# Decode attention over paged latents: pages turned by VectorE and scored in 32x32 tiles, with a fourth page buffer and loads shared by SyncE and GpSimd's gathers

## The reference, cut to what matters

```python
# cache_ckv (160, 128, 256), cache_kpe (160, 128, 32), page_table (8, 16)
c_past = cache_ckv[page_table].reshape(8, 2048, 256)
kpe_past = cache_kpe[page_table].reshape(8, 2048, 32)
s = einsum('bqhr,bkr->bhqk', q_lat, c_past) + einsum('bqhe,bke->bhqk', q_pe, kpe_past)
p = softmax(s * 96 ** -0.5)          # with the new token's own key beside the past ones
o_lat = einsum('bhqk,bkr->bqhr', p, c_past)
o = einsum('bhqr,rhv->bqhv', o_lat, w_uv);  x = x + o.reshape(b, n, 1024) @ w_o
```

## Time and profile before

| | |
|---|---|
| median of 3 executions | 2004.9 us (2004.75 to 2006.88) |
| the profiled execution | 2008.5 us, its span 2006.8 us |
| TensorE busy | 1965.1 us (98% of the span) |
| VectorE, ScalarE, GpSimd busy | 1280.1, 820.4, 132.3 us |
| mean granted TensorE clock | 0.988 of full |
| scores of request 0 done, scores of request 7 done | 1510.23 us, 1575.93 us of the span |

### The profile page before, as it was taken

How to read it: one execution, slowest core, us unless ns; L and a number is a source line. 1 busy time by engine, 2 the same in 40 slices (tenths; PEclk the granted TensorE clock), 3 DMA queues, 4 the chain that set the end, 5 groups by cost and what they waited for, 6 DMA issues and landing times.

```text
span 2006.8 us, 41571 instructions
## 1 busy us (share of the span) xinstructions
PE 1965.1 (98%) x17584; PEld 1878.2 (94%) x17584; DVE 1280.1 (64%) x1781; ACT 820.4 (41%) x1243; POOL 132.3 (7%) x231
## 2 busy tenths in 40 slices
PE   8999999998999999999999999999989999999998
PEld 7999999988999999999999999997656899999998
DVE  6445486697469577576875856655764349668474
ACT  5332233343245244355452534554654244345252
POOL 3002002010000000000000000000048000000000
PEclk9999999989999999999999999998999999999999
DMA  7233234864342322234322322231248422323222
GB/s 150 85 102 88 77 91 115 278 134 97 95 137 85 124 87 98 72 105 116 97 87 83 126 89 87 78 101 51 53 119 234 151 70 79 127 85 125 86 74 75
DMA packets 260625, 211.49 MB, mean 105 GB/s; under 512 B 42372, under 2 KB 235426, under 8 KB 260450
## 3 DMA queue, kind: packets, MB, share of 16 engines
q1 hardware_dynamic: 248528, 187.52, 31.6%
q0 software_dynamic: 6656, 13.69, 2.4%
q10 hardware_dynamic: 5266, 7.78, 1.2%
HBM read 195.22 MB, written 10.33 MB: 102 GB/s over the span
## 4 chain that ended last, share of the span: by engine, by line
PE 68%; DVE 3%; ACT 2%; issue 2%; SPq 1%; DMA 0%; DVEq 0%; ACTq 0%
PE ps L2459 25%; PE ps L2487 25%; PE ps L2388 6%; PE ps L2401 2%; PE ps L3034 1%; PE ps L2941 1%; PE ps L3190 1%; PE ps L3067 1%; SPq L637 1%; PE ps L3011 1%; PE ps L2835 1%; SPq L652 1%; DVE wl L1666 0%; DVE xl L1617 0%; DVE mx L2210 0%
## 5 line engine op out<-in xcount | busy, mean ns | idle before, releaser
L2388 PE MATMUL ps<-xh,wh 128*128 128x260 f32 x1088 | 286.9, 285 | 2.6 <-DVE xl L1617 1.4
L2388 PE MATMUL ps<-xl,wh 128*128 128x260 f32 x1088 | 283.7, 283 | 0.0
L2487 PE MATMUL ps<-xoh,wh 128*128 128x260 f32 x992 | 281.3, 284 | 1.3 <-DVE sq L1833 1.3
L2487 PE MATMUL ps<-xoh,wl 128*128 128x260 f32 x992 | 281.0, 283 | 0.0
L2487 PE MATMUL ps<-xol,wh 128*128 128x260 f32 x992 | 280.6, 283 | 0.0
L2459 PE MATMUL ps<-xh,wh 128*128 128x260 f32 x872 | 228.8, 284 | 0.6 <-DVE wl L1666 0.6
L1065 ACT ACTIVATE wh<-rw 128x1024 fp32r<-128x1024 f32 (+1 forms) x135 | 138.8, 1029 | 218.6 <-PE ps L2459 151.7
L2459 PE MATMUL ps<-xl,wh 128*128 128x260 f32 x872 | 227.0, 282 | 0.0
L2388 PE MATMUL ps<-xh,wl 128*128 128x260 f32 x1088 | 219.3, 283 | 0.0
L988 ACT ACTIVATE wh<-raw 128x1024 fp32r<-128x1024 f32 (+1 forms) x90 | 100.5, 1116 | 283.0 <-PE ps L2388 251.2
L2388 PEld LDWEIGHTS ps<-xh,wh 128*128 128x128 f32 x1088 | 205.6, 189 | 6.9 <-issue 3.9
(11 more groups left out here) (550 smaller groups left out, 4214.9 us busy)
## 6 DMA issues: line engine op xcount, KB each, us to landing
rw<-ffn_w_gate SPq DMA_DIRECT2D x33, 1024.0 KB, 5.3
rw<-ffn_w_up SPq DMA_DIRECT2D x33, 1024.0 KB, 7.9
rw<-ffn_w_down SPq DMA_DIRECT2D x12, 2048.0 KB, 7.7
raw<-ffn_w_gate SPq DMA_DIRECT2D x22, 512.0 KB, 3.8
raw<-ffn_w_up SPq DMA_DIRECT2D x22, 512.0 KB, 3.7
raw<-ffn_w_down SPq DMA_DIRECT2D x16, 704.0 KB, 4.8
rw<-ffn_w_down SPq DMA_DIRECT2D x6, 1536.0 KB, 6.6
cb<-cache_ckv SPq DMA_DIRECT2D x72, 128.0 KB, 3.9
```

The costliest lines, as they stand in the source:

```text
L2388: got = mm(ps[0:width, bank + half, 0:HALF], w[par_][:, k * width:k * width + width], src[:, k0 + k, half * HALF:half * HALF + HALF], star ...
L2487: got = mm(ps[:, bank + mat, T0], w[:, cols], src[:, j, k, :], start=first and k == 0 and m == 0 and s == 0, stop=k == 3 and m == 1, skip_ ...
```

## The change

* **Turning.** The 36 transposes of TensorE for each request and the nine copies out of PSUM go. VectorE turns the pages in SBUF with its own transpose, which works on 32x32 blocks: one instruction over 512 numbers a partition for the keys (into `kbT`) and four over 1024 numbers a partition for the latents (chunk c into `cbT[:, c-1]`, 64 of the 256 latent numbers each). The semaphore `d_t` now counts these.
* **Scoring.** A 32x32 block leaves 32 latent numbers on the partitions of each of four quarters, and each quarter holds other positions. So the scores are made of tiles with 32 rows and 32 columns, all 16 of the array: `past_scores(b, c)` issues 16 matmuls of 128 columns for the keys (c = 0) and 32 for each of the four latent chunks, 144 for a request. Each quarter of rows writes a PSUM bank of its own (banks 0 to 3, which request b+1 may write only when the exponential of request b has read them). The queries are needed on every quarter: GpSimd writes them to DRAM once and reads them back eight times (`dr_q`, `qrep`).
* **Order.** TensorE's order for a request is now: transposes of the probabilities, all scores of request b+1, weighted sum of request b. The copy of the turned probabilities moves from VectorE to ScalarE; ScalarE's copy of the weighted sum comes one request later.
* **Pages.** A page lies on 32 partitions with four positions on each, so that a partition receives 4 KB of latents or 512 bytes of keys. SyncE issues 8 latent pages and 4 key pages for a request; GpSimd gathers the others with indirect DMAs of four pages each (2 for latents, 3 for keys) whose row numbers it works out once from the page table.
* **Buffers.** A fourth latent buffer `cbw` lies over `wh[0]`, `wh[1]` and part of `wl[0]`. Therefore the splitting of the `w_o` blocks 0 and 1 leaves the prompt's steps 4 and 6 and comes with the blocks 2 and 3 at the end of the decode loop (`wide_hi`, `wide_lo`, into the first two page buffers). `uv` moves to `cbT` and is loaded when the last scores are done.

```diff
-            def turned(b, q):
-                dve.wait_ge(d_t, b * 9 + q + 1)
+            def turned(b, c):
+                if c == 0:
+                    dve.wait_ge(d_key[b % KB_BUFS], KEY_0[b % KB_BUFS] + (b // KB_BUFS + 1) * 16 * SP_KEYS)
+                    dve.wait_ge(d_gkey[b % KB_BUFS], (b // KB_BUFS + 1) * 16 * (NQ - SP_KEYS // NQ))
+                elif c == 1:
+                    dve.wait_ge(d_in[b % CB], IN_1 + (b // CB + 1) * 16 * SP_PG)
+                    dve.wait_ge(d_gin[b % CB], (b // CB + 1) * 16 * (NQ - SP_PG // NQ))
                 if b >= 1:
-                    dve.wait_ge(d_s, b)
-                copy(cbT[:, q // 4, (q % 4) * 512:(q % 4) * 512 + 512], ps[:, (0, 1, 7)[(b * 9 + q) % 3], :]).then_inc(d_td, 1)
+                    dve.wait_ge(d_s, (NCT + 1) * (b - 1) + c + 1)
+                if c == 0:
+                    V.transpose(kbT, kb[b % KB_BUFS].rearrange("p g e -> p (g e)")).then_inc(d_t, 1)
+                else:
+                    V.transpose(cbT[:, c - 1, :, :].rearrange("p q (g u) -> p g q u", u=HP),
+                                cb[b % CB][:, :, 2 * HP * (c - 1):2 * HP * c].rearrange("p g (q r) -> p g q r", q=2)).then_inc(d_t, 1)
...
             for b in range(NB):
-                dve.wait_ge(d_s, b + 1)
-                own(V.tensor_reduce(mb[:, b:b + 1], ps[:, 2 + b % 2, :], AX.X, ALU.max))
+                if b + 1 < NB:
+                    turned(b + 1, 0)
+                dve.wait_ge(d_s, (NCT + 1) * (b + 1))
+                own(V.tensor_reduce(mb[:, b:b + 1], ps[:, 0:NQ, 0:P], AX.XY, ALU.max))
                 ts(nmb[:, b:b + 1], mb[:, b:b + 1], -SCALE, None, ALU.mult).then_inc(d_m, 1)
                 if b + 1 < NB:
-                    turned(b + 1, 1)
-                    turned(b + 1, 3)
-                else:
-                    wide_lo(0)
-                dve.wait_ge(d_pt2, b + 1)
-                if b >= 1:
-                    dve.wait_ge(d_o, b)
-                copy(pbT[:, :, :], ps[:, 4, :].rearrange("p (m q) -> p m q", m=NQ)).then_inc(d_pe, 1)
+                    for c in range(1, NCT + 1):
+                        turned(b + 1, c)
+                if b >= NB - 2:
+                    wide_lo(b - NB + 2)
...
+            def past_scores(b, c):
+                if b == 0 and c == 0:
+                    pe.wait_ge(d_qr, 16 * (1 + 2 * NQ))
+                if b >= 1 and c == 0:
+                    pe.wait_ge(d_e, b)
+                pe.wait_ge(d_t, (NCT + 1) * b + c + 1)
+                for q in range(2 if c else 1):
+                    n = 2 * (c - 1) + q
+                    for a in range(NQ):
+                        rows = slice(HP * a, HP * a + HP)
+                        w, keys_ = (qrep[n // NQ][rows, n % NQ, b, :], cbT[rows, c - 1, q, :]) if c else (qpe[rows, b, :], kbT[rows, :])
+                        for j in range(NQ):
+                            got = mm(ps[HP * j:HP * j + HP, a, 0:P], w, keys_[:, P * j:P * j + P],
+                                     start=c == 0, stop=c == NCT and q == 1, skip_group_check=True)
+                got.then_inc(d_s, 1)
...
+            def gather(src, dst, b, g, arrived):
+                G.indirect_dma_start(dst[:, ROWS * g:ROWS * (g + 1), :].rearrange("p v r -> p (v r)"), None,
+                                     inp[src].rearrange("n (u v) r -> (n u) (v r)", v=ROWS),
+                                     bass.IndirectOffsetOnAxis(ap=rows_of[:, NQ * b + g:NQ * b + g + 1], axis=0)).then_inc(arrived, 16)
```

More of the change, by code:

```diff
@@ L922, in rope_rows, with number, keys, pages @@
                     sp.dma_start(qs[DN:DQ, 2 * (i % 2) + h, :], qq[r0:r0 + DR, NH // 2 + i // 2, 0:SEQ]).then_inc(a_qs[i % 2], 16)
[L924 removed]
+            numbers = {}
+            def number(b):
+                numbers[b] = [sp.value_load(pt[0:1, b * NPG + g:b * NPG + g + 1], min_val=0, max_val=NPOOL - 1) for g in range(SP_PG)]
+            def keys(b):
+                keys_free(sp, b)
+                for g in range(SP_KEYS):
+                    sp.dma_start(page(kb[b % KB_BUFS], g), inp["cache_kpe"][bass.ds(numbers[b][g], 1)].rearrange(
+                        "a (u v) r -> (a u) (v r)", v=ROWS)).then_inc(d_key[b % KB_BUFS], 16)
+            def pages(b):
+                latents_free(sp, b)
+                for g in range(SP_PG):
+                    sp.dma_start(page(cb[b % CB], g), inp["cache_ckv"][bass.ds(numbers[b][g], 1)].rearrange(
+                        "a (u v) r -> (a u) (v r)", v=ROWS)).then_inc(d_in[b % CB], 16)
+            sp.wait_ge(d_pt, 16)
             sp.wait_ge(q_ev, NQT)
@@ L943, in _ @@
             load(WO0 + 1, (WO0 + 1) % 2, wo[:, :, P:2 * P], KD)
-            caches()
-            sp.wait_ge(d_o, NB - 2)
+            for b in range(NB):
+                pages(b)
+                if b == 0:
+                    keys(0)
+                if b == 1:
+                    for m in range(AHEAD, NB):
+                        number(m)
+                if b + 1 < NB:
+                    keys(b + 1)
+            for d in range(2, 4):
+                load(WO0 + d, (WO0 + d) % 2, wo[:, :, d * P:d * P + P], KD)
+            sp.wait_ge(d_s, (NCT + 1) * NB)
             sp.dma_start(uv[:, :, :], uvd).then_inc(d_uv, 16)
-            for d in range(2, KD - 2):
+            for d in range(4, KD - 2):
                 load(WO0 + d, (WO0 + d) % 2, wo[:, :, d * P:d * P + P], KD)
@@ L3166, in _ @@
                 turned_probs(i, 3)
-                if not more:
-                    turned(0, 0)
                 turned_probs(i, 4)
-                if not more:
-                    turned(0, 1)
                 turned_probs(i, 5)
@@ L3218, in _ @@
+            for c in range(NCT + 1):
+                past_scores(0, c)
+            for b in range(NB):
                 pe.wait_ge(d_e, b + 1)
```

283 lines of the change are left out of this document (149 added, 134 removed).

## The result

The changed kernel takes 2032.8 us (median, 2030.2 to 2036.9) against 2005.9 for the kernel before on the same chip: ratio 1.0134, 95% interval 1.0111 to 1.0158. It is **1.3% slower**, where 17.4 us less were forecast. Its profiled execution took 2036.9 us, span 2035.0, against 2008.5 and 2006.8 before, so the traces differ by 28.2 us.

A forecast was written before the change was run, and what follows sets the result against it. TensorE was taken to bound the decode loop, VectorE after the change. Loop -20.5, start -0.5, tail +2.6, 1 given back: -17.4, so 1991.1 profiled and 1987.5 us as median; own range 1982 to 1994, over all 1981 to 2010.

The forecast's parts named there:

- the scores' price: Decode loop, TensorE: score records start 8 ns apart, so 0.5 us a chunk and 2.3 us for a request's scores.
- The packing: Score matmuls: 16 tiles of 32x32 work side by side, 8 ns a record, continued from one and four tiles.
- VectorE's chain: Decode round: maximum, four latent transposes, then TensorE's last chunk; sum 6.35 us, taken as 6.45, the new bound.
- the 20.5 us: Decode loop: gain forecast for the seven rounds between requests' last scores, 45.2 us instead of 65.7.
- TensorE before: Decode loop of the kernel before: TensorE sets the round, 9.37 us a request, 4.4 of it turning pages.
- close second bound: Decode loop of the kernel before: page loads bound next after TensorE, DMA share 0.83 at 234 GB/s.
- VectorE: Decode loop: VectorE's page transposes take 1.18 us a latent chunk, 4.7 for four, and 0.6 for the keys.
- Gathers: Page loads beside the loop: each GpSimd gather taken at 1.0 us, 0.54 the bound below.
- Start: Up to request 0's scores: done at 1509.7 against 1510.2, 0.5 us less, within 2 either way.
- Tail: Behind the last scores: uncovered wait, less filler before the `w_uv` product and four later steps, 2.6 us more.
- that the tiles do not pack: Rival, scores: records start 30 ns apart, round 11.3 us, 2026 us, slower; decides from 22 ns; chance 0.14.
- The falling clock: Rival, decode loop: TensorE idles and its clock falls to 1.2 GHz, round 8.6 us, 2005 us, same; chance 0.08.

The follow-up runs named there:

- few loads: Changed kernel without the latents' page loads of requests 4 to 7, their key pages loaded as before: 2020.3 us, ratio 1.0064.
- few scores: Changed kernel with 102 instead of 288 score records a request, three quarters of the latents' scores left out: 1993.8 us, ratio 0.9945.

## Why the prediction was wrong, step by step

* **The step that failed** is the scores' price: "records of 16 columns in four column tiles start eight in 0.06 us, 8 ns each, so they can be issued that fast", and from it 0.5 us a chunk and 2.3 us a request. It took a rate from a burst for a rate that lasts. The groups in the earlier trace rows are bursts of 8, 64 and 128 records, and 128 are exactly one packet; the loop has 324 records a round. One packet takes 3.47 us with the DMA engines idle and 7.04 to 9.4 in the changed kernel's stretches under loads, so 324 / 128 = 2.53 packets bound the round at 8.8 us with the first figure and 17.8 with 7.04. The first figure alone leaves 0.6 us a round of the 2.9 that were forecast; the mean round was 13.1.
* **The packing**, "a continuation of one and four tiles", was mis-sized as well. The keys' records start 9.7 ns apart, the latents' 15 (1537.12 to 1539.05) and, with few loads, 13 (128 from 1578.42, last start at 1580.05). As an estimate from these, a request's scores are 0.3 + 256 x 13 to 15 ns = 3.6 to 4.1 us and not 2.3, and the last chunk 0.8 to 1.0 and not 0.5. With every instruction at hand VectorE's chain would then be 6.7 to 6.8 us instead of 6.35, and 2 to 3 of the 20.5 us would still be lost. Why the latents' records stand wider apart than the keys' was not tried.
* **What the stalls account for.** 26.7 of the 27.6 us fall between the first and the last exponential. Without them the seven rounds would be 64.9 us, 9.3 each, where 6.45 were forecast. The wider records and the clock (below) have a part in that gap; how much each was not separated.
* **TensorE before**: 9.37 us a round, bound by TensorE: right (12 transposes of 0.13 us raised it to 10.97, and 64 records to 9.97). But the "close second bound" was nearer than taken: 0.55 us less in TensorE's round made pages late.
* **VectorE**: four transposes 4.7 us, key transpose 0.6. Measured 4.62 (20 of `L2269` in 23.1 us, one behind the other) and 0.67 to 0.70. Right. With few scores, where VectorE sets the pace, four rounds ran at 6.0 to 7.0.
* **Gathers** taken at 1.0 us: 0.95 (median of `L3451`), 1.26 apart. No transpose waited for a page in the changed kernel. Right, though a loop at 6.45 us would have tested the loads far harder, and the long rows' price (5.7 us on the kernel before) was not in the sum.
* **Start**: -0.5 forecast. The first exponential came 4.7 later. Some 2.4 of that lies before the decode work. Executions whose instructions are the same up to there differ by more (a group of the prompt's attention started at 1442.2 in the changed kernel and at 1438.3 in the run with few scores), so no effect of the change can be read from it. From that group to the first exponential it is 73.8 us, against 71.6 before: 2.2 more, with stalls of 1.1 and 0.9 for "issue" in it.
* **Tail**: +2.6 forecast. From the last scores to the `w_uv` product it is 16.7 us against 15.5, but the product itself is shorter (3.64 against 4.85), and from the last exponential to the end the changed kernel needs 2.5 less. Neither `d_uv` nor `d_ws` was waited for late. Mis-sized, by less than a measurement tells.
* **The rivals**: that the tiles do not pack was given 2026 us and 0.14, and its time is near, by luck: its 30 ns a record, or the 22 from which it decides, are not there (9.7 and 13 to 15 ns). The falling clock came (0.53 in 1517 to 1534, 0.72 over the rounds with loads) behind the stalls: TensorE stalls, and then runs the weighted sum in 3.64 us instead of 1.93. It adds to rounds where no packet is due; how much of the 26 us is its own was not separated.
* What slows a packet beside page loads was not tried by itself. Its own transfer hardly does: 1.28 us in the stretch of 7.04 against 1.03 in the one of 3.47. The time goes by before it starts: 4.45 us behind the last stall's end against 1.05. "DMA: Bandwidth & Descriptors" of the Trainium skill, section "Queues, rings and completion order", has each DMA engine take its queues in turn, a packet at a time; the later start with more bytes beside it agrees with that, but it stays an argument.

## What to carry to other kernels

Count a loop's instructions as well as its columns: TensorE's records and weight loads divided by 256 are packets, and a packet needs 3.5 us at best and 7 to 9 beside heavy loads here, so below some 27 ns a record (3.47 us / 128), on average over a packet, the engine starves, however well small tiles pack. Beside loads the limit lies higher and depends on them: with rows of 1 KB a round of 9.97 us for 194 records (51 ns each) had no stall and one of 14.0 for 322 (44 ns) did. A rate read from a burst of at most 128 records says nothing about this, and a stall "issue" inside a group of equal records, 128 apart, is its sign. Before taking time off an engine that sets a loop, look at how far the next bound is: here it was 0.5 us away in the loads, and it took another buffer to get at the rest.

## What the runs showed of the hardware

* TensorE's instruction supply: 256 instructions each 3.47 us with the DMA engines idle (share 0.02). In the changed kernel beside loads 7.04 us twice (shares 0.82 and 1.03) and 9.40 once (0.71). A stall ends 1.3 to 1.7 us behind the end of its instruction packet.
* 32x32 tiles of 128 columns, float32, at full clock: records 9.7 ns apart for the keys, 13 to 15 ns for the latents.
* Rows of 4 KB into 32 partitions keep the DMA engines busier than rows of 1 KB into 128: share 1.04 against 0.83 at the same 230 GB/s, and 5.7 us lost for it.
* VectorE's 32x32 transpose of 128x1024 float32 takes 1.21 us, 1.16 from start to start; a gather of 128 rows occupies GpSimd 0.95 us.
